# Two projections in rounded products, with their operands split inside the norm

## The reference, cut to what matters

```
h = modulate(rmsnorm(x, n1), sh1, sc1)             # 384 x 1024
a_q, a_k, a_v, b_q, b_k, b_v, z, xbc, dt_raw = split(h @ w_in)
#   1536 columns of "rows" (a, b, z), 768 of xbc, 16 of dt_raw (step sizes)
xbc = silu(conv_centred(xbc, conv_w, conv_b))      # 3 taps along the tokens
dt  = softplus(dt_raw + dt_bias)
mod = silu(c) @ w_ada + b_ada                      # 6 x 1024, for two conditionings
```

## Time and profile before

| | us |
|---|---|
| median of 3 runs (819.85 to 822.02) | 821.7 |
| the profiled execution | 819.76 |
| its span, first to last instruction | 817.9 |
| TensorE / VectorE / ScalarE busy | 758.9 / 586.0 / 476.9 |
| mean granted TensorE clock | 0.984 of full |

### The profile page before, as it was taken

One profiled execution on the slowest core, in us unless ns is written; L12 is line 12 of the kernel. 1 busy time (PEld: TensorE's weight loads), 2 busy tenths in 40 slices (PEclk: granted clock), 3 DMA queues, 4 the chain that ended last, 5 costly groups with the idle time before them and its releaser, 6 DMA issues.

```text
span 817.9 us, 10722 instructions
## 1 busy us (share of the span) xinstructions
PE 758.9 (93%) x3980; PEld 571.8 (70%) x3980; DVE 586.0 (72%) x934; ACT 476.9 (58%) x768; POOL 49.7 (6%) x36
## 2 busy tenths in 40 slices
PE   4997989999989999999989998988997799999995
PEld 2565878457945888888766787745793688888874
DVE  4229676884558789999663866688544988999965
ACT  3033883575355777777542388357534687777752
POOL 0000641000000000000000064100000000000000
PEclk9999999999999999999999999999998999999998
DMA  9952032978347899999760113285830179999912
GB/s 368 422 186 75 30 128 60 419 294 310 104 155 308 289 374 358 372 363 370 270 273 12 58 46 129 104 339 177 303 109 0 52 268 377 357 376 371 360 51 80
DMA packets 33488, 185.98 MB, mean 227 GB/s; under 512 B 5136, under 2 KB 6288, under 8 KB 16400
## 3 DMA queue, kind: packets, MB, share of 16 engines
q1 hardware_dynamic: 33424, 185.16, 60.2%
HBM read 182.53 MB, written 2.62 MB: 226 GB/s over the span
## 4 chain that ended last, share of the span: by engine, by line
PE 79%; DVE 11%; ACT 5%; issue 4%; DMA 1%; DVEq 0%; SPq 0%; ACTq 0%
PE psum L739 22%; PE psum L854 11%; PE psum L768 11%; PE psum L1056 8%; PE psum L825 7%; PE psum L791 3%; PE psum L620 2%; PE psum L1070 1%; DVE att L1930 1%; PE psum L817 1%; PE psum L924 1%; PE psum L717 1%; PE psum L1026 1%; PE psum L661 1%; PE psum L752 1%
## 5 line engine op out<-in xcount | busy, mean ns | idle before, releaser
L1726 DVE TENSOR_TENSOR split<-ring,split 128x2048 fp32r<-128x2048 f32 x96 | 219.9, 2291 | 27.6 <-ACT split L1319 25.0
L1319 ACT CAST split<-ring 128x2048 fp32r<-128x2048 f32 x96 | 183.4, 1911 | 18.1 <-PE psum L768 14.5
L739 PE MATMUL psum<-split,y_hi 128*128 128x512 f32 x512 | 162.7, 399 | 0.0
L739 PEld LDWEIGHTS psum<-split,y_hi 128*128 128x128 f32 x512 | 93.7, 188 | 19.6
L739 PE MATMUL psum<-split,y_lo 128*128 128x512 f32 x256 | 100.6, 393 | 0.0
L854 PE MATMUL psum<-ring_r,hT_hi 128*128 128x512 f32 x216 | 74.0, 397 | 2.7 <-ACT qkT L1413 2.4
L768 PE MATMUL psum<-split,hidT 128*128 128x512 f32 x256 | 70.3, 396 | 1.8 <-DVE hidT_lo L1731 1.8
L825 PE MATMUL psum<-hT,ring 128*128 128x384 f32 x192 | 69.2, 499 | 0.0
L768 PEld LDWEIGHTS psum<-split,hidT 128*128 128x128 f32 x256 | 47.4, 187 | 14.5 <-DVE hidT_lo L1731 3.6
L2120 POOL TENSOR_TENSOR ud<-const,da_hi 128x1024 fp32r<-128x1024 f32 x12 | 30.7, 2578 | 431.8 <-DVE da_lo L1823 431.3
L739 PEld LDWEIGHTS psum<-split,y_lo 128*128 128x128 f32 x256 | 48.0, 188 | 11.1
(11 more groups left out here) (258 smaller groups left out, 1339.0 us busy)
## 6 DMA issues: line engine op xcount, KB each, us to landing
ring<-in_w_gu SPq DMA_DIRECT2D x64, 1024.0 KB, 5.0
ring<-in_w_ada SPq DMA_DIRECT2D x40, 1024.0 KB, 6.7
ring<-in_w_down SPq DMA_DIRECT2D x32, 1024.0 KB, 5.2
ring<-in_w_rows SPq DMA_DIRECT2D x12, 1024.0 KB, 5.1
ring<-in_first SPq DMA_DIRECT2D x8, 1024.0 KB, 14.7
ring<-in_w_out SPq DMA_DIRECT2D x8, 1024.0 KB, 4.8
ring<-in_w_xbc SPq DMA_DIRECT2D x8, 784.0 KB, 8.4
par<-in_par SPq DMA_DIRECT2D x1, 1632.0 KB, 11.9
```

The lines of the kernel that those rows point to most:

```text
L739: last = pe.matmul(dst, x[:, g, t, :], w[:, j, :], start=(t == 0 and i == 0), stop=(t == KD - 1 and i == 2))
L1319: act.copy(splits[n % SPLITS][:, 0, :], slot(key)).then_inc(raised("whi", l, p), 1)
L1726: tt(lo, slot(unit_key(l, p, n)), hi.bitcast(F32), ALU.subtract).then_inc(raised("wlo", l, p), 1)
```

## The change

- The products of step xbc become three rounded ones for each k and chunk, x_hi*h_hi, x_lo*h_hi and x_hi*h_lo. Those of the step sizes become two for each tile: hT_hi by 32 columns (high and low part of the weights side by side) and hT_lo by the 16 high ones. VectorE adds the two halves of the result.
- The xbc weights are split too: ScalarE writes x_hi (a new tile, under others that are used later) and dt_w, VectorE writes x_lo over the weights in the ring.
- x is split chunk by chunk, inside the norm (`split_h(l, k)`), and the weights at four places there and in xbc (`split_x(l, i)`). The three first `split_win` move behind them, into step xbc.
- The two pieces h_hi are listed at the head of xbc's pieces, in slots H_AT and H_AT + 1; the xbc pieces go where the list's rule puts them.

```diff
-    s = [("norm", 0)] + ada[:early] + [("w_split", 0), ("h_split", 0), ("w_split", 1), ("h_split", 1), ("w_split", 2), ("xbc",)]
+    s = [("norm", 0)] + ada[:early] + [("xbc",)]
@@ pieces
             if s[0] == "xbc":
+                pieces += [("h_hi", l, 0), ("h_hi", l, 1)]
                 if l == 0:
                     pieces.append(("first", 0, 0))
                 for i in range(KD // 2):
                     pieces.append(("xbc", l, i))
                     if l == 0:
                         pieces += [("first", 0, j) for j in (2 * i + 1, 2 * i + 2) if j < KD]
-                pieces += [("win", l, p) for p in range(5)] + [("w_hi", l, 2), ("win", l, 5), ("w_hi", l, 4), ("h_hi", l, 0),
-                                                               ("h_hi", l, 1), ("w_hi", l, 5)]
+                pieces += [("win", l, p) for p in range(5)] + [("w_hi", l, 2), ("win", l, 5), ("w_hi", l, 4), ("w_hi", l, 5)]
@@ held_by
-                        ("w_hi", l, 4): ("win", l, 1), ("w_hi", l, 5): ("xbc", l, 2),
-                        ("h_hi", l, 0): ("xbc", l, 0), ("h_hi", l, 1): ("xbc", l, 1)})
+                        ("w_hi", l, 4): ("win", l, 1), ("w_hi", l, 5): ("xbc", l, 2)})
@@ slots
-        elif key[0] == "xbc" and key[2] < 2:
-            b = H_AT + 1 - key[2]
+        elif key[0] == "h_hi":
+            b = H_AT + key[2]
@@ tensor, step xbc
                         for i in range(KD // 2):
-                            pe.wait_ge(*landed(("xbc", l, i)))
+                            pe.wait_ge(*in_lo(l, f"x{i}"))
                             for kk in range(2):
                                 k = 2 * i + kk
-                                pe.wait_ge(*modulated(l, 0, k))
+                                pe.wait_ge(*in_lo(l, f"h{k}"))
                                 for m in range(TILES):
-                                    last = pe.matmul(dtd[:, m * DT:(m + 1) * DT], hT[:, k, m * P:(m + 1) * P],
-                                                     w[:, kk, XBC:XBC + DT], ...
+                                    pe.matmul(dtd[:, 2 * m * DT:2 * (m + 1) * DT], hT_hi[:, k, tok], dt_w[:, k, :], ...
+                                    last = pe.matmul(dtd[:, 2 * m * DT:(2 * m + 1) * DT], hT_lo[:, k, tok], dt_w[:, k, 0:DT], ...
                                 for c in range(6):
-                                    last = pe.matmul(bank(("xbc", l, c))[:, 0:TOK], w[:, kk, c * P:(c + 1) * P], hT[:, k, :],
-                                                     start=(k == 0), stop=(k == KD - 1))
+                                    for j, (w, x) in enumerate(((x_hi[:, k, part], hT_hi), (x_lo(l, i)[:, kk, part], hT_hi),
+                                                                (x_hi[:, k, part], hT_lo))):
+                                        last = pe.matmul(bank(("xbc", l, c))[:, 0:TOK], w, x[:, k, :], ...
@@ scalar
+            def split_x(l, i):
+                act.wait_ge(*landed(("xbc", l, i)))
+                act.copy(x_hi[:, 2 * i:2 * i + 2, :], src[:, :, 0:XBC])
+                act.copy(dt_w[:, 2 * i:2 * i + 2, 0:DT], src[:, :, XBC:XBC + DT]).then_inc(sig["in_hi"], 1)
+            def split_h(l, k):
+                if k == 0:
+                    for i in range(2):
+                        if former_in["h_hi", l, i]:
+                            act.wait_ge(*release[former_in["h_hi", l, i]])
+                act.wait_ge(*modulated(l, 0, k))
+                act.copy(hT_hi[:, k, :], hT[:, k, :]).then_inc(sig["in_hi"], 1)
@@ scalar, norm (layer 1; layer 0 does this beside its copies in step xbc)
+                    if not n:
+                        split_h(l, c)
+                        if c == 3:
+                            split_x(l, 1)
@@ scalar, step norm
+                            split_x(l, 0)
                         ...
                         norm(l, arg[0])
@@ scalar, step xbc
+                        if l == 0:
                             for j in range(KD):
                                 key = ("first", 0, j)
                                 act.wait_ge(*full(key))
                                 act.copy(ada_rows[:, 0:2 * P], bank(key)[:, 0:2 * P]).then_inc(*was_read(key))
+                                split_h(0, j)
+                                if j % 2 and j < KD - 1:
+                                    split_x(0, (j + 1) // 2)
+                        else:
+                            split_x(l, 2)
+                            split_x(l, 3)
+                        for p in range(3):
+                            split_win(l, p)
@@ vector, norm
+                if l < DEPTH and not n:
+                    split_x(l, 0)
@@ vector, norm of layer 1: behind the scaling of its part (k = 0; 1 to 3; 4 to 7)
+                    if l and not n and c0 == 1:
+                        split_h(l, 0)
+                    if l and not n and c0:
+                        for c in range(c0, c1):
+                            split_h(l, c)
+                        for i in (1,) if c0 == 1 else (2, 3):
+                            split_x(l, i)
@@ vector, norm of layer 0: behind the modulation of chunk c
+                        if not (l or n):
+                            split_h(0, c)
+                            if c % 2 and c < KD - 1:
+                                split_x(0, (c + 1) // 2)
@@ vector, step xbc
                     elif kind == "xbc":
+                        for p in range(3):
+                            split_win(l, p)
...
-                            if c == 2:
-                                dve.wait_ge(*release["xbc", l, KD // 2 - 1])
-                                split_h(l, 1, KD - 2, KD)
```

More of the change, by code:

```diff
@@ L404, in build @@
             cbd = sb("cbd", [P, 2], c=mix)
+            with ExitStack() as ahead_of_masks:
+                x_hi = sb("x_hi", [P, KD, XBC], F32R, c=ahead_of_masks)
+                dt_w = sb("dt_w", [P, KD, 2 * DT], F32R, c=ahead_of_masks)
             with ExitStack() as shared_late:
@@ L567, in spent, with x_lo @@
             return done[key][0], 1
-        IN_HI = {name: n + 1 for n, name in enumerate(("w0", "h0", "w1", "h1", "w2", "w3", "w4", "w5"))}
-        IN_LO = {name: n + 1 for n, name in enumerate(("w0", "h0", "w1", "h1", "w2", "h2", "w3", "w4", "w5"))}
+        IN_AT = [{name: n + 1 for n, name in enumerate(order)} for order in IN_ORDER]
         def in_hi(l, name):
-            return sig["in_hi"], per["in_hi"] * l + IN_HI[name]
+            return sig["in_hi"], per["in_hi"] * l + IN_AT[l][name]
         def in_lo(l, name):
-            return sig["in_lo"], per["in_lo"] * l + IN_LO[name]
+            return sig["in_lo"], per["in_lo"] * l + IN_AT[l][name]
+        def x_lo(l, i):
+            return ring_r[:, place["xbc", l, i], 0:2 * (XBC + DT)].rearrange("p (k n) -> p k n", k=2)
         def win_hi(l, p):
@@ L824, in _ @@
                                         pe.wait_ge(*fill(("xbc", l, c)))
-                                    last = pe.matmul(bank(("xbc", l, c))[:, 0:TOK], w[:, kk, c * P:(c + 1) * P], hT[:, k, :],
-                                                     start=(k == 0), stop=(k == KD - 1))
+                                    part = slice(c * P, (c + 1) * P)
+                                    for j, (w, x) in enumerate(((x_hi[:, k, part], hT_hi), (x_lo(l, i)[:, kk, part], hT_hi),
+                                                                (x_hi[:, k, part], hT_lo))):
+                                        last = pe.matmul(bank(("xbc", l, c))[:, 0:TOK], w, x[:, k, :],
+                                                         start=(k == 0 and j == 0), stop=(k == KD - 1 and j == 2))
                                     if l == 0 and c == 1 and k + 1 < KD:
@@ L1343, in _ @@
                             squares(l, 1, range(3, KD))
-                        elif not l:
-                            squares(0, 0)
+                        else:
+                            if not l:
+                                squares(0, 0)
+                            split_x(l, 0)
                         if not (l or arg[0]):
@@ L1348, in _ @@
                         norm(l, arg[0])
-                        if not (l or arg[0]):
+                    elif kind == "ada" and arg[2] == KD - 1:
+                        ada(arg[0], arg[1])
+                    elif kind == "w_split":
+                        split_win(l, arg[0])
+                    elif kind == "xbc":
+                        if l == 0:
                             for j in range(KD):
@@ L1757, in _ @@
                         split_win(l, arg[0])
-                    elif kind == "h_split":
-                        dve.wait_ge(*release["xbc", l, 1 + arg[0]])
-                        split_h(l, arg[0], 4 * arg[0], 4 + 2 * arg[0])
                     elif kind == "xbc":
+                        for p in range(3):
+                            split_win(l, p)
                         if l == 0:
```

69 lines of the change are left out of this document (35 added, 34 removed).

## The result

The changed kernel takes **841.07 us** (median, 839.15 to 841.55) against 820.78 for the kernel before on the same chip (819.03 to 822.02): ratio 1.0244, interval 1.0217 to 1.0272. It is 20.3 us slower. The forecast was 9.4 us slower (830, range 823 to 836): the sign was right, the time lies above the range. The profiled execution has a span of 839.5 us against 817.9.

The account below looks back on a forecast made before the run. TensorE, busy 93% and 79% of the chain, was taken as the main bound, with other limits in some stages. Terms -1.4 - 3.5 + 7.2 + 7.1 = +9.4 gave 829.2, or 831.1 from the median; forecast 830, 8 in 10 from 823 to 836.

Parts of the forecast that it names:

- Sign and slots: Slower overall; adaLN loads behind the rows wait for the high part's slots, scores 7.2 and 7.1 us late (layers 0, 1).
- Start of layer 0: Constants ahead of the first weights, then splits, put the first product near 20.8 us, 3.2 late.
- Products end 3.2 - 6.8 = 3.6 earlier: Layer 0's products start 3.2 us late, save 6.8, so end near 60.8; 1.4 remains at the rows.
- The clock: Lower level costs 1.7 us in layer 0's rows, repeating; as much again per layer possible ahead of scores, only in range.
- the price of a product: Per layer 48 f32 products at 0.662 us become 144 rounded ones at 0.174: 6.8 us less.
- The sequence at the end: Layer 0's first row product waits for the step-size bank behind three weight splits; rows start near 67.5, not 68.88.
- Layer 1 gains 6.8 - 1.7 - 1.6 = 3.5: Layer 1: products save 6.8 us, less 1.7 for a later first product and 1.6 for a late third weight piece.
- The split of the first weights lies in the wait for the sums: Layer 1's norm: that split fits in an existing wait, so the first product comes only 1.7 us late.
- (a): Rival, scores: the wait for adaLN loads is absorbed, leaving only -4.9 us, 815 to 817; chance 0.08.
- (b): Rival, scores: half the wait is absorbed by later waits, 3.5 us per layer, 822 to 825; chance 0.12.
- (c): Rival: late splits starve the products, layer 0 gains nothing, clock falls once more, 833 to 836; chance 0.11.
- The six narrow rounded products per k: Step-size products, xbc stage: still six records per k, no change taken; bounds 4.6 us gained to 3.8 lost per layer.

Follow-up runs that it names:

- e3_const: Changed kernel, first adaLN loads behind the rows sent to earlier-free slots, constants and parameters loaded behind the first weights again: 825.52 us.
- e5_dt_first: Changed kernel, VectorE splits the first row weights, reads the step-size sums, only then splits the other two: 841.94 us.
- e8_rows: Changed kernel, adaLN loads in earlier-free slots, second and third row-weight splits moved behind the convolutions of chunks 1 and 3: 829.89 us.
- e4_warm: Changed kernel, adaLN loads in earlier-free slots, six useless f32 products ahead of layer 1's first xBC product: 829.47 us.
- e7_norm: Changed kernel, adaLN loads in earlier-free slots, norm steps ordered ahead of weight splits on ScalarE and VectorE, both layers: 827.11 us.
- e11_norm1: e3_const plus, in layer 1 alone, the norm order of e7_norm and the six useless products of e4_warm: 820.96 us.
- e10_warm0: e3_const plus eight useless f32 products in layer 0's idle time ahead of the first row product: 822.26 us.

## Why the prediction was right or wrong

**Sign and slots: right.** The step that decided the forecast, the high part at the head of the list and the first adaLN loads in exactly these slots, held in place, cause and size: 6.9 and 7.0 after against 7.2 and 7.1, and 14.8 when put into the kernel before alone. The third load landed 9.9 behind the release where I had put 11.1, and the block behind it, with the clock at 0.75 around it, took the difference back; that the sum still fits is luck. The estimate from the Trainium skill (DMA: Bandwidth & Descriptors, "Anatomy of one DMA") was 9.2, nearer to the measured 9.9 than my row. The page gives its fit for transfers that GpSimd issues, and here SyncE issues them.

**Start of layer 0: right** (first product 20.63 against 20.8 forecast), and the constants were named as a cause; taking them back gave 1.8 us. The terms listed there add up to 20.4, so 0.4 of the 20.8 had no source.

**"Products end 3.2 - 6.8 = 3.6 earlier", layer 0: wrong.** Rows started 1.3 later instead of 1.4 earlier. I treated the delay at the start as a shift of the whole. The clock was put at nothing in this stretch, and it was 0.74 over 17 to 30, where it was 1.00 before: up to 3.4 us of products. The products gained 2.8 us from the first to the last instead of 6.8; in e3_const, with the clock at 1.00, they gained 5.3. So the price of a product was nearly right (0.181 us where the rounds are full, not 0.174, 1.0 us more per layer), and the clock's term was missing. With the constants back, rows started 3.4 us earlier on average, for 1.7 at the first product. The sequence at the end, where rows wait for VectorE's three splits, was read rightly (5.4 us of wait). And a start of the rows that is earlier only by VectorE's order is worth nothing at their end, as e5_dt_first and e8_rows show: VectorE's work behind the products has to be done earlier too.

**"Layer 1 gains 6.8 - 1.7 - 1.6 = 3.5": wrong, and the largest miss.** It lost 4.7. Three parts: (1) "The split of the first weights lies in the wait for the sums" failed. What lies there is time in which the engines issue nothing, 4.22 us of "issue" on VectorE before and 3.29 on ScalarE after, and the split begins only behind it (429.17); VectorE's scaling starts 6.9 us behind the last residual sum, where it started 4.9 behind it, and the first product comes at +4.1, not +1.7. In the code a long conditional body is skipped at this place, and the only transfers in ScalarE's gap are three packets of the instruction queues; that the skipping makes the gap was not tested. (2) The third scaling stood behind the second split in VectorE's queue and held the bank of the sums that the sixth chunk wants. I had counted that order for the weights (1.6 us) and not looked at the bank. (3) The clock was at 0.60 over the 7.8 us from the first product and at 0.72 over the next 6.2, behind an idle time of 4.17 us ahead of the first product and the bank wait of 1.4, and the sum had no term for it. e4_warm, e7_norm and e11_norm1 take them apart: in the stage the useless products alone lose 2.2 us, the order alone gains 3.0, both gain 4.3. With both, from the first product to the last one less the wait that is left, the products take 31.0 us, 5.5 less than before.

**The clock** was named in the prediction for the idle time ahead of layer 0's rows, and left in the range for that ahead of the scores. In the two stages of products it was put at nothing, and that was the error of method. Measured, it cost about 2.6 us in layer 0's products (changed kernel against e3_const) and 1.0 in the block ahead of the scores (1.94 against 0.90); in layer 1 it can't be priced apart from the bank wait.

**Rivals.** (a) and (b) fell with the distances to the scores. (c) came nearest, with a layer 0 that gains nothing and one more fall of the clock, but for another reason: no round of layer 0 waited for a late piece of weights (TensorE's waits behind the first product add up to under 0.2 us). No rival had the loss in layer 1.

## What to carry to other kernels

TensorE time that is saved counts only if TensorE stays fed: work out for each stretch which engine comes next, and put a term for slow products behind each new idle time of TensorE. When a buffer's entry is moved in a list that a placement rule reads, work the rule through for what comes after its last use. When one wait is taken away, read which bank or buffer the same instruction wants next before a gain is put down.

## What the runs showed of the hardware

- A TensorE that is listed as busy can still be at its lower clock. With two of three products left out the granted clock stood at 0.58 and 0.50 while TensorE was listed as busy 94% and 98%, and in layer 1 144 products at 0.18 us became 48 at 0.353: 26 us became 17, not 9.
- Useless products in idle time paid where the products behind them were on the path: eight of them brought the 72 row products from 18.50 to 16.79 us (kernel before) and from 19.68 to 17.04 (e10_warm0), and the last row product came 1.0 and 2.6 us earlier. Where a wait stood behind the warmed products, they paid nothing (e4_warm).
- The six narrow rounded products per k (16 and 32 columns) took 0.55 us, 0.11 apart, where six records of f32 took 0.57 before, as forecast.
